# The warming products behind six norms get other shapes: 512, 128, 256, 384, 512 and 256 columns

## The reference, cut to what matters

```python
for i in range(DEPTH):                                   # DEPTH = 2
    f = swiglu(rms_norm(h, ln_ffn1[i, 0]), ffn1_w_gu[i], ffn1_w_down[i])
    h = h + 0.5 * rms_norm(f, ln_ffn1[i, 1])
    hn = rms_norm(h, ln_mix[i, 0])
    m = short_conv_mixer(...) if i % 2 == 0 else diff_attention_mixer(...)
    h = h + rms_norm(m, ln_mix[i, 1])
    f = swiglu(rms_norm(h, ln_ffn2[i, 0]), ffn2_w_gu[i], ffn2_w_down[i])
    h = h + 0.5 * rms_norm(f, ln_ffn2[i, 1])
```

## Time and profile before

| | |
|---|---|
| time, median of 3 executions | 1368.21 us (1368.03 to 1368.21) |
| span of the profiled execution | 1366.7 us |
| TensorE products busy | 1353.4 us, 99% of the span |
| weight loads of TensorE busy | 1327.8 us, 97% |
| DVE busy | 901.7 us, 66% |
| ACT busy | 662.8 us, 48% |
| mean granted clock of TensorE | 0.998 |

### The profile page before, as it was taken

How to read it: one execution, slowest core, us unless ns; L and a number is a source line. 1 busy time by engine, 2 the same in 40 slices (tenths; PEclk the granted TensorE clock), 3 DMA queues, 4 the chain that set the end, 5 groups by cost and what they waited for, 6 DMA issues and landing times.

```text
span 1366.7 us, 26805 instructions
## 1 busy us (share of the span) xinstructions
PE 1353.4 (99%) x11002; PEld 1327.8 (97%) x11002; DVE 901.7 (66%) x1374; ACT 662.8 (48%) x962; POOL 13.5 (1%) x27
## 2 busy tenths in 40 slices
PE   9999999999999999999999999999999999999997
PEld 9999999999999999999999999999999999999997
DVE  6666548768666548666548997866655767777543
ACT  5443535446444535434545666644445545644332
POOL 0000000000000000000000000000001000000000
PEclk9999999999999999999999999999999999999999
DMA  8555553334545533545553323455655513455550
GB/s 296 176 183 196 206 184 139 139 131 148 185 167 205 200 135 122 187 159 214 188 193 119 124 93 124 155 184 184 242 179 192 201 62 124 155 185 184 185 186 31
DMA packets 30271, 227.68 MB, mean 167 GB/s; under 512 B 3472, under 2 KB 4944, under 8 KB 6384
## 3 DMA queue, kind: packets, MB, share of 16 engines
q1 hardware_dynamic: 28912, 224.14, 46.2%
q0 software_dynamic: 720, 1.82, 0.4%
q10 hardware_dynamic: 560, 0.61, 0.2%
HBM read 225.49 MB, written 1.06 MB: 166 GB/s over the span
## 4 chain that ended last, share of the span: by engine, by line
PE 93%; DVE 4%; ACT 1%; issue 1%; DVEq 0%; POOL 0%; ACTq 0%; POOLq 0%
PE ps L1926 26%; PE ps L1928 26%; PE ps L1927 26%; PE ps L1968 1%; PE ps L2008 1%; PE ps L1963 1%; PE ps L1996 1%; PE ps L1964 1%; PE ps L1994 1%; PE ps L1942 1%; PE ps L2249 1%; PE ps L2496 1%; PE ps L1974 0%; PE ps L2497 0%; PE ps L2498 0%
## 5 line engine op out<-in xcount | busy, mean ns | idle before, releaser
L554 ACT ACTIVATE w_hi<-w_raw 128x2048 fp32r<-128x2048 f32 (+2 forms) x175 | 374.1, 2138 | 376.3 <-PE ps L1928 362.3
L1926 PE MATMUL ps<-x_hi,w_hi 128*128 128x272 f32 (+1 forms) x1920 | 552.5, 288 | 0.1
L1928 PE MATMUL ps<-x_hi,w_lo 128*128 128x272 f32 (+1 forms) x1920 | 549.3, 286 | 0.0
L1927 PE MATMUL ps<-x_lo,w_hi 128*128 128x272 f32 (+1 forms) x1920 | 547.7, 285 | 0.0
L1093 DVE TENSOR_TENSOR w_lo<-w_raw,w_hi 128x2048 fp32r<-128x2048 f32 (+2 forms) x163 | 413.1, 2534 | 199.5 <-ACT w_hi L554 199.4
L1926 PEld LDWEIGHTS ps<-x_hi,w_hi 128*128 128x128 f32 x1920 | 361.8, 188 | 4.4 <-issue 3.3
L1928 PEld LDWEIGHTS ps<-x_hi,w_lo 128*128 128x128 f32 x1920 | 361.9, 188 | 0.0
L1927 PEld LDWEIGHTS ps<-x_lo,w_hi 128*128 128x128 f32 x1920 | 361.6, 188 | 0.1
L1926 PE MATMUL ps<-hid_hi,w_hi 128*128 128x272 f32 (+1 forms) x960 | 274.3, 286 | 0.2 <-DVE w_lo L1093 0.2
L1928 PE MATMUL ps<-hid_hi,w_lo 128*128 128x272 f32 (+1 forms) x960 | 273.6, 285 | 0.0
L1927 PE MATMUL ps<-hid_lo,w_hi 128*128 128x272 f32 (+1 forms) x960 | 272.8, 284 | 0.0
(11 more groups left out here) (338 smaller groups left out, 1531.6 us busy)
## 6 DMA issues: line engine op xcount, KB each, us to landing
w_raw<-w_gu SPq DMA_DIRECT2D x86, 1024.0 KB, 4.9
w_raw<-w_dn SPq DMA_DIRECT2D x32, 1408.0 KB, 6.0
w_raw<-w_ff SPq DMA_DIRECT2D x32, 1024.0 KB, 4.9
w_raw<-w_conv_in SPq DMA_DIRECT2D x8, 1536.0 KB, 6.2
w_raw<-w_qkv SPq DMA_DIRECT2D x8, 1536.0 KB, 6.2
w_raw<-w_mix_in SPq DMA_DIRECT2D x8, 1536.0 KB, 6.3
w_raw<-w_conv_out SPq DMA_DIRECT2D x4, 1024.0 KB, 5.0
w_raw<-w_attn_out SPq DMA_DIRECT2D x4, 1024.0 KB, 4.9
```

The source lines that it names most:

```text
L554: act.activation(w_hi[j % SPLIT][:, 0:width], w_raw[j][:, 0:width], ACT.Copy).then_inc(hi_ready, 1)
L1926: pe.matmul(out_ap, w_hi[slot][:, cols], hi(k), start=first, stop=False)
L1927: pe.matmul(out_ap, w_hi[slot][:, cols], lo(k), start=False, stop=False)
L1928: mm = pe.matmul(out_ap, w_lo[slot][:, cols], hi(k), start=False, stop=last)
```

## The change

Each norm gets its own number and shape of warming products. A table has, for each u, the count, the stationary columns and the columns that stream. The tiles that they read are the same, now over two chunks where 512 columns are wanted.

```diff
+        WARM = {0: (13, P, 512), 1: (25, P, P), 2: (13, 64, SEQ), 3: (13, P, 384), 4: (12, P, 512), 5: (13, 32, SEQ)}
...
-                warm = y_hi[:, 0, :] if u == 1 else z_hi[:, 0, :] if u == 4 else hid_hi[:, first_col(u):T]
-                for _ in range(4 if u in APART else 22):
-                    pe.matmul(ps[:, 2 if u in APART else 5, 0:warm.shape[-1]], warm[:, 0:P], warm, start=True, stop=True)
+                warm = y_hi[:, 0:2, :].rearrange("p k t -> p (k t)") if u == 1 else z_hi[:, 0:2, :].rearrange("p k t -> p (k t)") \
+                    if u == 4 else hid_hi[:, first_col(u):]
+                count, rows, width = WARM[u]
+                for _ in range(count):
+                    pe.matmul(ps[0:rows, 2 if u in APART else 5, 0:width], warm[:, 0:rows], warm[:, 0:width], start=True, stop=True)
```

## The result

The changed kernel takes 1371.45 us (median of 10, 1371.15 to 1371.69) against 1368.2 of the kernel before on the same chip. The ratio is 1.0024, with a 95% interval of 1.0015 to 1.0034: slower by 3.25 us. The prediction was 1371.2.

A forecast was written before the change was run, and what follows sets the result against it. TensorE was taken to bound the kernel, so added products count beyond what it already loses waiting: 1.59, 1.00 and 0.65 us, less 0.2, make 3.0 us on the 1368.21 median, giving 1371.2 us, range 1369.8 to 1373.0.

The forecast's parts named there:

- What bounds the kernel: Whole kernel: TensorE, 93% of the chain; added products count in full except where it waits, as for DVE in the entry.
- S: Behind each norm: what TensorE already loses from first warming product to entry's end, 0.87 to 1.19 us, gained back if late.
- E: At each norm: what new warming products take more than the old; delay is E - S, or nothing where S is larger.
- The prices: Per warming product: 0.228 us for 512 columns, 0.173 for 384, 0.107 for 128, 0.1174 for 256.
- The 0.2 us given back behind u = 3: Of 0.65 us delay behind u = 3, DVE is made late by 0.35 to 0.5, so 0.2 is taken off.
- The wait for `v_tok`: In the attention: TensorE's 1.0 us wait was to become 0.1 to 0.3 us shorter.
- The sum: All norms: 1.59 + 1.00 + 0.65 = 3.24 us, less 0.2 given back, taken as 3.0 us.
- Cheap 128-column products (2): Rival at u = 1: 128-column products stream at 0.059 us, so u = 1 costs nothing; 1370.2; 15%.
- A pace that does not depend on the columns (3): Rival on prices: load and issue set about 0.125 us per product whatever the width; 1.7 us, 1369.9; 8%.
- Only the first gap given back (4): Rival in the entries: DVE and ACT fall behind with TensorE, only the first gap returns; 7.3 us, 1375.5; 9%.
- The clock (5): Rival behind u = 2 and u = 5: narrow products drop the clock to 1.2 GHz, 0.5 us per such microsecond; 3%.
- That the time falls (6): Rival for the whole kernel: the time falls through something not seen; no size given; 3%.

The follow-up runs named there:

- u0_only: Kernel before with only the u = 0 norm changed, to 13 warming products of 512 columns; 1369.91 against 1368.24 us.
- doses_b: Kernel before with 26 products of 512 columns (u = 0), 50 of 128 (u = 1), 13 of 256 (u = 2, 5); 1376.79 against 1368.19 us.
- none_apart: Kernel before without warming products behind u = 0, 1, 2, 3 and 5, u = 4 kept; 1368.12 against 1368.24 us.
- doses_a: Kernel before with u = 0, 1, 2, 3, 5 given 6, 25, 25, 26, 25 products of 512, 128, 64, 384, 128 columns; 1372.01 against 1368.19 us.
- u4_narrow: Kernel before with 46 products of 128 columns, 32 stationary, in place of 22 of 256 at u = 4; 1368.38 against 1368.14 us.
- none_at_all: Kernel before without warming products at any of the six norms, u = 4 included; 1369.93 against 1368.24 us.
- u4_half: Kernel before with 6 products of 512 columns in place of 22 of 256 at u = 4; 1369.52 against 1368.14 us.
- u4_quarter: Kernel before with 3 products of 512 columns in place of 22 of 256 at u = 4; 1369.60 against 1368.14 us.

## Why the prediction was right

**What bounds the kernel** held. TensorE's delay counts in full outside the waits, which u0_only and doses_b show at one and at two times the dose, and DVE sets the pace of the entry, which none_apart shows from the other side. One reading was off without harm: the chain through the entry has three operations of DVE per chunk, L1290, L1284 and L1160, which take 1.11 us together in the trace, and not four; the `w_lo` of L1237 in the earlier trace rows is one piece of 1.13 us behind the last chunk. Nine products at 0.1254 us take 1.13, so the comparison of the two engines stands.

**S**, what TensorE loses behind each norm anyway, was the step that carried most, and it was read from plain differences of starts and not from the view of waits, which lists at most 0.2 us for TensorE's products at any of these five norms; asked for the weight loads, the same view lists 0.5 to 0.9. doses_a put a dose of E = 0.88 us against S = 0.87 at u = 0, and the entry ended at its old place. At u = 2 and u = 5 E stayed below S, at no cost. What came back was 0.88 us at u = 0 in the change, 1.13 for 1.18 at u = 1 and 1.04 for 1.10 at u = 3.

Here luck had a part. The price of 0.1254 us is 35 us over 279 products, but a window counts every product that is in flight in it, and only 277 of them start in these 35 us, which makes 0.126 (and 0.118 for the 0.1174 of 256 columns). With 0.126 the S of u = 0 would have been 0.8. The entry itself runs at the lower price: in the changed kernel, without a gap, its 60 products behind u = 0 take 223.32 - 215.80 = 7.52 us, 0.1253 each.

**The prices.** 512 columns measured (215.80 - 212.83) / 13 = 0.228 us (0.228 taken), 384 columns 0.174 (0.173). 128 columns measured 0.110 (0.107 taken), which is 0.06 of the 0.11 us by which u = 1 came out above the forecast; the other 0.05 is its S. The reason taken, that the weight load sets the pace, fits doses_a, which shows that the stationary side does. 256 columns with 64 stationary ones cost 0.113 instead of 0.117, which was below S either way.

**The 0.2 us given back behind u = 3** were 0.25. DVE was made late as described: its read of L1944's result now waits for TensorE, in the timeline of DVE after the change:

```profile
741.01 0.44 DVE L1169 TENSOR_SCALAR h_sum<-ps 128x272 f32<-128x272 f32 x1 [0.37 <-PE ps L1944]
```

TensorE was 2.54 us late when it began the warming products there (730.02 - 727.49, to 0.01), so this read would have stood at 740.54 and is 0.47 us late, inside the 0.35 to 0.5 given. With four times the excess in doses_a the same read waits 2.63 us, and again 0.25 is given back in the attention:

```profile
741.57 0.44 DVE L1169 TENSOR_SCALAR h_sum<-ps 128x272 f32<-128x272 f32 x1 [2.63 <-PE ps L1944]
```

So this cover is no reserve of its own; it is worth what lies between the two engines at that read. In the change DVE stands 741.01 - 738.00 = 3.01 us late there and TensorE 3.25, and the difference is what came back; in doses_a it is 3.57 against 3.80.

One detail was off. The wait for `v_tok` was to shorten by 0.1 to 0.3 us, and it went only from 1.01 to 0.93, first before and then after the change:

```profile
768.88 0.33 PE L2233 MATMUL ps<-sq,a_sb 128*128 128x128 f32 x1 [1.01 <-ACT v_tok L776]
...
771.88 0.33 PE L2237 MATMUL ps<-sq,a_sb 128*128 128x128 f32 x1 [0.93 <-ACT v_tok L778]
```

The other 0.17 of the 0.25 us came back earlier, at a short gap ahead of a weight load that the view of TensorE's products has not. The load at 752.33 us of before starts when the `w_lo` of DVE ends (751.07 + 1.22). In the changed kernel DVE is 3.01 us late with it and TensorE was 3.25, so that the load no longer waits, and TensorE is 3.08 us late from there on. DVE and the load, before and then after:

```profile
751.07 1.22 DVE L1182 TENSOR_TENSOR w_lo<-w_raw,w_hi 128x1024 fp32r<-128x1024 f32 x1
752.33 0.19 PEld L1926 LDWEIGHTS ps<-x_hi,w_hi 128*128 128x128 f32 x1
...
754.08 1.21 DVE L1184 TENSOR_TENSOR w_lo<-w_raw,w_hi 128x1024 fp32r<-128x1024 f32 x1
755.41 0.19 PEld L1928 LDWEIGHTS ps<-x_hi,w_hi 128*128 128x128 f32 x1
```

**The sum.** 3.24 us were forecast for the norms and 3.45 measured, 0.2 us given back and 0.25 measured. The misses are of one sign, 0.11 at u = 1, 0.07 at u = 3 and 0.03 at u = 5, and small.

**The rivals.** Cheap 128-column products (2) fell to the measured 0.110. A pace that does not depend on the columns (3) fell to 0.228 us for 512 columns. With it fell, for products of this format, the rule of the Trainium skill, "TensorE: Matmul & The Clock Gate", section "Back-to-back issue gap", which states about 0.131 us for 512 columns. Only the first gap given back (4) fell: all gaps of the entry behind u = 0 went. The clock (5) stayed at 1.00 in the changed kernel, and u4_narrow shows that narrow products keep it. That the time falls (6) is out with 3.25 us more.

No version beats the kernel before: none_apart, which leaves out the products that do nothing, is equal to it.

## What to carry to other kernels

Filler work in front of a wait is free up to a knee and costs in full past it, so the knee is what to work out: the time from the filler to the end of the stretch, less the number of products in it times their usual distance. This is longer than the waits that the profile lists, because it holds the small gaps too. It can be counted on where, as here, another engine goes through the stretch at a pace of its own and does not wait for the filled one. Give each filler a reason as well: of six places here only the one with 4 us to fill needs it, and there half the cover costs 1.4 us, nearly the 1.7 of none. And price a product by both its sides: here a short product with a full stationary side cost 0.110 us with 128 streaming columns and 0.108 with 64, and one of 512 columns cost 0.228.

## What was not expected of the hardware

- A product in this split format costs 0.060 us with 128 streaming and 32 or 64 stationary columns, 0.108 to 0.110 with 64 or 128 streaming and 128 stationary ones, 0.174 with 384 and 0.228 with 512 streaming columns. The last two are 0.118 plus the added columns at 2.4 GHz (0.171 and 0.225) to 0.003 us, so the columns past 256 stream at about the full clock; between 256 and 272 columns the windows show 0.0005 us for a column, a fifth more than that.
- 64 stationary columns made 256-column products a little faster (0.113 us) than either 32 (0.118) or 128 (0.119). No run says why.
- The granted clock fell at another place of the gap in each of three traces. In none_at_all it still stood at 1.00 in a stretch of 2 us with no product (856 to 858 us) and fell at 859.2, when products were under way again. In u4_half it fell 0.1 us ahead of the first product, and in u4_quarter at 857.2, 1.3 us ahead of it, and there it stayed low twice as long. In all three the loss of time falls on the work behind the wait. Gaps of 1.4 and 1.6 us between two starts kept the clock, gaps of 2.9, 3.6 and 4.2 us lost it.
